# Chunk-band attention of layer 1: logits from split queries and keys, and late transposes in the output bank

## The reference

```python
def _band_attend(q, k, v, q_pos, k_pos, rel_table):
    rel = jnp.clip(q_pos[:, None] - k_pos[None, :], -REL_CLIP, REL_CLIP) + REL_CLIP
    bias = jnp.moveaxis(rel_table[rel], -1, 0).astype(F32)
    logits = jnp.einsum('bthd,bshd->bhts', q, k).astype(F32) * (DH ** -0.5) + bias[None]
    logits = jnp.where((k_pos >= 0)[None, None, None, :], logits, -jnp.inf)
    p = jax.nn.softmax(logits, axis=-1)
    return jnp.einsum('bhts,bshd->bthd', p.astype(v.dtype), v)
```

## Time and profile before

| what | value |
|---|---|
| median of the runs | 2955.19 us |
| the profiled execution | 2956.45 us, its span 2954.6 us, mean granted PE clock 0.98 |
| PE busy | 2824.2 us (96%) |
| POOL busy | 1530.0 us (52%) |
| attention of layer 1 | from 1913.72 us to about 2131 us of the span |

### The profile page before, as it was taken

How to read it: one execution, slowest core, us unless ns; L and a number is a source line. 1 busy time by engine, 2 the same in 40 slices (tenths; PEclk the granted TensorE clock), 3 DMA queues, 4 the chain that set the end, 5 groups by cost and what they waited for, 6 DMA issues and landing times. The chain is left out here.

```text
span 2954.6 us, 61044 instructions
## 1 busy us (share of the span) xinstructions
PE 2824.2 (96%) x24967; PEld 2635.7 (89%) x24967; DVE 1722.6 (58%) x3113; ACT 998.7 (34%) x2105; POOL 1530.0 (52%) x1382
## 2 busy tenths in 40 slices
PE   6999999997799999999999999999999999999998
PEld 4869999665699999999999999866699999999998
DVE  6389999556647633436797300066648544346785
ACT  3241111456525333333232201266525333333232
POOL 2222223664524877777576233144334777776675
PEclk8999999997999999999999999999999999999999
DMA  6736762733241122124322232263211222214322
GB/s 222 243 122 227 263 234 74 226 132 120 74 155 51 66 87 83 70 87 139 103 81 75 72 105 96 71 218 102 89 70 41 84 77 76 87 66 138 124 70 70
DMA packets 192389, 339.12 MB, mean 115 GB/s; under 512 B 27992, under 2 KB 107632, under 8 KB 190256
## 3 DMA queue, kind: packets, MB, share of 16 engines
q1 hardware_dynamic: 138832, 266.50, 26.9%
q10 hardware_dynamic: 53280, 68.72, 6.8%
HBM read 268.30 MB, written 79.49 MB: 118 GB/s over the span
## 5 line engine op out<-in xcount | busy, mean ns | idle before, releaser
L758 POOL TENSOR_TENSOR ah_ring_lo<-ah_raw,ah_ring_hi 128x512 fp32r<-128x512 f32 (+2 forms) x426 | 578.7, 1366 | 238.0 <-ACT ah_ring_hi L1182 146.9
L109 PE MATMUL tr_acc<-tr_quad_hi,ah_ring_hi 128*128 128x264 f32 x2432 | 694.5, 286 | 7.7 <-ACT tr_kept L1193 2.6
L111 PE MATMUL tr_acc<-tr_quad_hi,ah_ring_lo 128*128 128x264 f32 x2432 | 693.1, 285 | 0.0
L110 PE MATMUL tr_acc<-tr_quad_lo,ah_ring_hi 128*128 128x264 f32 x2432 | 690.7, 284 | 0.0
L109 PEld LDWEIGHTS tr_acc<-tr_quad_hi,ah_ring_hi 128*128 128x128 f32 x2432 | 458.6, 189 | 9.5 <-ACT tr_kept L1193 3.0
L110 PEld LDWEIGHTS tr_acc<-tr_quad_lo,ah_ring_hi 128*128 128x128 f32 x2432 | 458.6, 189 | 0.1
L111 PEld LDWEIGHTS tr_acc<-tr_quad_hi,ah_ring_lo 128*128 128x128 f32 x2432 | 458.2, 188 | 0.0
L1827 DVE TENSOR_SCALAR_CACHE_REDUCE f_q<-score,choose_trial 128x384 bf16<-128x384 f32 (+6 forms) x224 | 242.2, 1146 | 1.1
L3035 DVE CUSTOM_DVE_ANT_0 pc_prob<-pc_dots,pc_bias 128x640 f32<-128x640 f32 (+4 forms) x128 | 79.0, 655 | 273.3 <-PE pc_dots L2897 272.5
L2151 POOL CAST f_w_hi<-f_raw 128x512 fp32r<-128x512 f32 x66 | 44.5, 675 | 359.9 <-DMA f_raw<-in_w_dram 236.0
L756 POOL CAST ah_ring_hi<-ah_raw 128x512 fp32r<-128x512 f32 (+1 forms) x114 | 72.7, 638 | 279.4 <-PE tr_acc L111 258.6
(11 more groups left out here) (420 smaller groups left out, 7338.7 us busy)
## 6 DMA issues: line engine op xcount, KB each, us to landing
f_ada_w<-in_w_ada_dram SPq DMA_DIRECT2D x48, 1024.0 KB, 7.5
scratch_inner<-tr_kept ACTq DMA_DIRECT2D x88, 264.0 KB, 2.2
ah_raw<-in_w_gate_dram SPq DMA_DIRECT2D x44, 512.0 KB, 3.5
ah_raw<-in_w_up_dram SPq DMA_DIRECT2D x44, 512.0 KB, 4.4
ah_raw<-in_w_down_dram SPq DMA_DIRECT2D x64, 256.0 KB, 3.1
f_raw<-in_w_dram SPq DMA_DIRECT2D x24, 512.0 KB, 9.7
out_z_dram<-f_stage ACTq DMA_DIRECT2D x60, 176.0 KB, 2.0
out_z_dram<-tr_value ACTq DMA_DIRECT2D x48, 176.0 KB, 2.0
```

What stands on the lines that cost most here:

```text
L109: pe.matmul(out, w_hi, hi, start=start, stop=False, skip_group_check=onto)
L110: pe.matmul(out, w_hi, lo, start=False, stop=False, skip_group_check=onto)
L111: return pe.matmul(out, w_lo, hi, start=False, stop=stop, skip_group_check=onto)
L758: pool.tensor_tensor(lo[:, 0:width], own, hi[:, 0:width].bitcast(F32), ALU.subtract).then_inc(w_ready, 1)
```

## The change

Only the attention of layer 1 (`joined`) changes in what it does; for layer 0 the waits come out as they were.

- From pair 1 on q and k are split into `q_hi`, `k_hi` (rounded) and `q_lo`, `k_lo` (the rest, over the raw tensor). POOL does this in four parts for the next pair, one behind each `weigh` of i = 3 to 6: a cast of 128x512 and a subtraction of 128x512. `mask_band` comes behind the first part.
- `scores` becomes `split_scores` for these pairs: three fp32r products for each head. A 640-key tile goes in two pieces of 320 columns, one in each bank; a 128-key tile is computed 256 wide. The first tile of a pair waits for the fourth part of its split.
- The third group of transposes moves from step s+2, behind the values, to the head of step s+3, in front of the first two groups of the next tile, and goes into `out[0]`; ACT copies it out at once, at the head of its step. The first two groups go one to ACT and one to DVE for every tile.
- On DVE `inverse` of tile s-1 moves from ahead of both logits to between them, and `finish` moves from the end of the step to its head. The probability buffers go from three tiles to four. The sample keys and values have one buffer instead of four.

```diff
+            def split(g, n):
+                b, at = g % 2, slice(T // 2 * (n // 2), T // 2 * (n // 2) + T // 2)
+                raw, hi, lo = ((q, q_hi, q_lo), (k, k_hi, k_lo))[n % 2]
+                if n == 0:
+                    pool.wait_ge(qk_in[b], 32 * ((g + 1) // 2))
+                    if g >= 3:
+                        pool.wait_ge(dots_done, dots_after[step_of["tile", TILES * (g - 1) - 1]])
+                pool.tensor_copy(hi[b][:, at], raw[b][:, at]).then_inc(split_hi, 1)
+                pool.wait_ge(split_hi, 4 * (g - 1) + n + 1)
+                pool.tensor_tensor(lo[b][:, at], raw[b][:, at], hi[b][:, at].bitcast(F32), ALU.subtract).then_inc(split_lo, 1)
+                pool.wait_ge(split_lo, 4 * (g - 1) + n + 1)
...
                 for u, (g, i) in enumerate(units):
                     weigh(u)
+                    if 3 <= i < 7 and g < pairs - 1:
+                        pool.wait_ge(weighed, 2 * u + 2)
+                        split(g + 1, i - 3)
                     if i == 3 and g < pairs - 1:
                         pool.wait_ge(weighed, 2 * u + 2)
                         mask_band(g + 1)
...
+            def split_scores(s):
+                u = tile(s)
+                g, i = units[u]
+                b, n = g % 2, keys[i]
+                first = P * (i + 1) - n
+                wide_by = 320 if in_halves(s) else max(n, 256)
+                for piece in range(2 if in_halves(s) else 1):
+                    for p, (left, right) in enumerate(((q_hi, k_hi), (q_hi, k_lo), (q_lo, k_hi))):
+                        for hd in range(2):
+                            half = slice(DH * hd, DH * hd + DH)
+                            at = at_dots(s) + 512 * piece
+                            last = pe.matmul(dots[hd][:, at:at + wide_by], left[b][half, P * i:P * i + P],
+                                             right[b][half, first + wide_by * piece:first + wide_by * piece + wide_by],
+                                             start=p == 0, stop=p == 2)
+                last.then_inc(dots_done, 1)
...
                 if i == 0 and g:
-                    pe.wait_ge(qk_in[b], 32 * ((g + 1) // 2))
+                    if joined:
+                        pe.wait_ge(split_lo, 4 * g)
...
+                if turn_place[n] == 2 and i == 4:
+                    pe.wait_ge(finished, u // 4)
...
             for s in range(last_of + 5):
                 if tile(s) is not None:
                     scores(s)
...
+                for j in late_turns(s - 3) if joined else ():
+                    turns(s - 3, j)
                 for j in range(min(turns_of(s - 2), 2)):
                     turns(s - 2, j)
...
-                for j in range(2, turns_of(s - 2)):
+                for j in () if joined else late_turns(s - 2):
                     turns(s - 2, j)
...
-                if mask is None and summed is not None:
-                    inverse(summed)
+                if ends_quad(s - 4) and joined:
+                    finish(tile(s - 4) // 4)
                 if tile(s) is not None:
                     logit(s, 0)
...
+                if joined and summed is not None:
+                    inverse(summed)
                 if both_first:
                     logit(s, 1)
```

More of the change, by code:

```diff
@@ L2588, in attention_phase @@
     quads = side.quads + [(side.blocks, side.blocks + 1)]
+    joined = mask is None
+    depth = 4 if joined else 3
     steps = []
@@ L2613, in turns_of, with late_turns @@
         return len(quads) if group(s) is not None else 0
+    def late_turns(s):
+        return range(2, turns_of(s))
     def sums_of(s):
@@ L2633, in attention_phase @@
             by_act.append(False)
+        for j in late_turns(s - 3) if joined else ():
+            turn_no[s - 3, j] = len(by_act)
+            by_act.append(True)
         for j in range(min(turns_of(s - 2), 2)):
             turn_no[s - 2, j] = len(by_act)
-            by_act.append((item(s - 2)[1] + j) % 2 == 0)
+            by_act.append(j == 0 if joined and tile(s - 2) is not None else (item(s - 2)[1] + j) % 2 == 0)
         if group(s - 3) is not None:
@@ L2648, in attention_phase @@
             by_act.append(True)
+    late_no = {turn_no[s, j] for s in range(last_of) for j in late_turns(s)} if joined else set()
+    turn_place, turn_before, held, plain_turns = [], [], {}, 0
+    for n in range(len(by_act)):
+        place = 2 if n in late_no else plain_turns % 2
+        plain_turns += n not in late_no
+        turn_place.append(place)
+        turn_before.append(held.get(place))
+        held[place] = n
     act_no = [sum(by_act[:n]) for n in range(len(by_act) + 1)]
@@ L2881, in dots_free, with in_halves, halves @@
                 pe.wait_ge(logits, sums_before[s - 1])
+        def in_halves(s):
+            return joined and units[tile(s)][0] > 0 and keys[units[tile(s)][1]] == 640
+        def halves(ap, n):
+            return ap.rearrange("p (b n) -> p b n", n=n)[:, :, 0:320]
         @block.tensor
         def _(pe):
+            def split_scores(s):
[13 more added lines that the diff above has]
+                last.then_inc(dots_done, 1)
             def scores(s):
@@ L2992, in side_values @@
                             right = s_v_new[:, 256 * g + DH * j:256 * g + DH * j + DH]
-                        last = pe.matmul(turn[n % 2][S * j:S * j + S, 0:DH], left, right, start=c == 0, stop=c == side.blocks)
+                        last = pe.matmul(turn_at(n)[S * j:S * j + S, 0:DH], left, right, start=c == 0, stop=c == side.blocks)
                 last.then_inc(turned, 1)
@@ L3145, in _ @@
                 for j in own:
-                    if j >= 2:
+                    if j >= 2 and not joined:
                         copy(s - 2, j)
-                if ends_quad(s - 4):
+                if ends_quad(s - 4) and not joined:
                     finish(tile(s - 4) // 4)
@@ L3218, in _ @@
                 own = [j for j in range(turns_of(s - 2)) if by_act[turn_no[s - 2, j]]]
+                for j in late_turns(s - 3) if joined else ():
+                    copy(s - 3, j)
                 for j in own:
```

86 lines of the change are left out of this document (54 added, 32 removed).

## The result

| | this kernel | kernel before |
|---|---|---|
| median of the runs | 2973.99 us (4 runs, 2972.24 to 2980.28) | 2954.68 us (4 runs, 2953.36 to 2957.77) |
| the profiled execution | 2975.20 us, span 2973.3 | 2956.45 us, span 2954.6 |
| attention of layer 1, first scores to first product of the next phase | 241.06 us | 221.27 us |
| the rest of the span | 2732.2 us | 2733.3 us |

The ratio of the times is 1.0068, with a 95% interval of 1.0057 to 1.0080: slower by 19 us. The forecast was 2972.5 in a range of 2959 to 2981, so the time came out as predicted; how much of that is luck stands in the part on the prediction. The whole difference lies in the stage that the change touches: it grew by 19.8 us, and the rest of the span did not grow.

A forecast was written before the change was run, and what follows sets the result against it. PE was busy 96%, but POOL's chain of weighs and split parts was taken to decide: 2956.45 + 8.1 + 9.2 (clock) = 2973.8 us for the profiled execution, 1.3 above the median, so 2972.5; range 2959 to 2981.

The forecast's parts named there:

- POOL's chain: Weigh(3) to part 4 keeps POOL busy 14.7 us; next pair's scores start 19.5 us after those of i = 3.
- The clock: Behind four new PE stops of 3.7 to 3.9 us the clock halves, costing 2.3 us each, +9.2 us.
- The sum without the clock: Layer 1 attention: POOL's delays less PE and DVE gains, summed over pairs and tail, +8.1 us.
- tail: End of the layer 1 attention stage, with its late groups of transposes joined: -0.3 us.
- PE and DVE alone: Steps i = 0 to 7 of a pair, without POOL's limit, would take 24.1 us against 25.2 before.
- The prices of scores and subtractions: Split scores of 640 keys take 1.08 us instead of 1.28; a POOL subtraction 1.28 us rather than 1.43.
- (a): Rival: PE's stops are there but the clock holds, 2963 us; chance 0.14.
- (b): Rival: POOL keeps up, so scores and transposes bring what they save, 2945 us; chance 0.07.
- (c): Rival: POOL's chain is shorter by a quarter and loss and gain cancel, 2955 us; chance 0.08.
- (d): Rival: fp32r products of the two heads run one after the other, 2988 us or more; chance 0.06.

The follow-up runs named there:

- e1_fill: Changed kernel, with PE turning the identity 35 times before the first scores of pairs 1, 3, 5 and 7: 2969.47 us, stage 233.25 us.
- e2_cheap: Changed kernel with POOL's subtraction replaced by a cheaper copy, so logits are not the reference's: stage 220.02 us.
- e8_act_casts: Changed kernel with the split's casts on ACT and POOL's subtractions behind weigh(2) to weigh(5) (pair 0: 3, 4, 4, 5): 2943.17 us, ratio 0.9964 to kernel before.
- e6_all_spread: Changed kernel with split parts behind weighs of i = 1, 2, 4, 5, for pair 0 behind 3, 4, 4, 5: 2948.78 us, ratio 0.9978 to kernel before.
- e7_all_spread_ahead: As e6_all_spread, with POOL's split of the next phase's weights moved from i = 0 to i = 7: 2949.55 us, ratio 0.9982 to kernel before.
- e4_inverse: Changed kernel with DVE's inverse back ahead of both logits: 2969.77 us, stage 235.36 us.
- e3_spread: Changed kernel with split parts behind weighs of i = 1, 2, 4, 5 from pair 1 on, pair 0 left alone: 2954.73 us (one execution), stage 217.55 us.

## Why the prediction was right, and where its terms were off

**POOL's chain (right).** I had 14.7 us from the start of weigh(3) to the end of part 4; it took 15.0. I had 19.5 us from the scores of i = 3 to the next pair's; it took 19.72 (1976.33 to 1996.05). The stops before pairs 1, 3, 5 and 7 measured 3.83, 3.84, 3.83 and 3.82 us, where I had 3.7 to 3.9, and those before pairs 2, 4 and 6 0.13 each. All are ended by the subtraction at L2894. Of the 0.3 us between 14.7 and 15.0, 0.2 are my rounding: 1.36 + 2.07 + 0.5 and three times 1.58 + 2.07 make 14.9.

**The clock (right in kind, near in size).** Behind the four stops the first step took 5.60, 5.32, 4.65 and 4.65 us instead of 3.03, and behind the first stop the second took 0.35 more: 8.5 us in all, where I had 4 x 2.3 = 9.2. I took 4.6 us of work at half clock behind each stop. The half-clock stretches were 6.8 us long before pairs 1 and 3 and 3.4 before pairs 5 and 7, and they did not begin where PE took up work again. Before pair 3 the clock fell 1.7 us ahead of that, while PE stood still; before pair 5 it was still 1.00 through the whole stop and fell 0.8 us behind it (windows of the kernel after, as above):

```profile
1994.40:1996.00 1.60, 0.00 (x0) 0.00 (x0) 0.00 (x0) 0.00 (x0) 1.51 (x2) 0.50 0.64 248
2051.10:2054.80 3.70, 0.00 (x0) 0.00 (x0) 0.00 (x0) 0.15 (x2) 3.45 (x5) 1.00 0.82 322
```

So a single stop cost 1.6 to 2.9 us, and that the average came near my 2.3 is partly luck. e1_fill gives nearly the same number from the other side (7.8). That the clock falls behind each of these four waits is what the section that I cited from the Trainium skill ("TensorE: Matmul & The Clock Gate", "HAM oscillation — how this bites in real kernels") says of a loop that waits in each round, and here the trace agrees. The waits of its example are longer than the stops of e2_cheap, 1.63 to 1.88 us, and behind those the clock fell in two of four.

**The sum without the clock (undersized).** It was to be +8.1 us and is 19.8 - 8.5 = +11.3. From the starts of each pair's first scores in both timelines, the clock's share taken off:

| | forecast | measured |
|---|---|---|
| pair 0 | +2.0 | +3.7 |
| pairs 2, 4, 6, each | +3.0 | +3.4 |
| pairs 1, 3, 5, each | -0.5 | -0.25 |
| pair 7 | -1.1 | -1.4 |
| tail | -0.3 | -0.4 |

The largest miss of a single pair is pair 0. I added the chain to pair 0's weigh(3) where the trace of before has it. But the move of `inverse` holds in pair 0 too and costs it 1.2 us: weigh(3) starts 2.40 us after the scores of i = 4 (1919.16 to 1921.56), in the kernel before 1.18 us (1921.53 to 1922.71). For the other pairs I had counted this move. Its step i = 3 was 0.15 us longer too. The rest is the chain, 0.3 us longer each time, and turns that wait for a late weigh: i = 7 of an odd pair takes 3.93 us, where I had 3.82, and i = 0 behind the sample step 3.50. The sample step itself was forecast right (3.9, measured 3.92).

**Luck in the total.** The stage was to grow by 17.3 us and grew by 19.8: 3.2 more without the clock, 0.7 less through it. The profiled execution came out 1.4 us above my 2973.8 and not 2.5, because the rest of its span happened to be 1.1 us shorter, and two misses in the stage went against each other. The mechanism was right; the closeness of the total is partly chance.

**PE and DVE alone (right, seen in e8_act_casts).** With POOL out of the way the steps of an ordinary pair take 3.03, 3.03, 2.88, 2.43, 2.88, 2.91, 3.12 and 3.56 us, 23.8 in all; I had 24.1. The inverse between the logits I priced at 0.15 us; in i = 4 it costs 0.07. DVE's timeline of the kernel after shows this: the reciprocal starts together with the read of the accumulator, and the second logit 0.07 us behind both, before the 0.16 us of the reciprocal are over.

```profile
1980.70 0.08 DVE L3120 DVE_READ_ACCUMULATOR2_ANT pc_least<- 128x1 f32 x1
1980.70 0.16 DVE L3138 RECIPROCAL pc_inv<-pc_sum 128x2 f32<-128x2 f32 x1
1980.77 0.80 DVE L3120 CUSTOM_DVE_ANT_0 pc_prob<-pc_dots,pc_bias 128x640 f32<-128x640 f32 x1
```

Where the reciprocal has to wait for ACT's row sum it costs more: in i = 5 of the same pair the logits start 1.06 us apart (1982.83 to 1983.89) instead of 0.75. The values of i = 2 wait 0.26 us for the copy of the late transposes (forecast 0.34); that step came out at its forecast all the same, and why i = 3 is 0.07 shorter than forecast stays open. The 9 to 10 us of gain that I had for this case are 10.0 in e8_act_casts, but not pair by pair: pairs 2 to 7 gain 1.4 to 1.7 us each, where I had 1.1 to 1.4, and pair 1 gains nothing because of its stop.

**The prices of scores and subtractions (right).** Scores of 640 keys hold PE 1.08 us (1988.21 to 1989.29). The subtraction takes 1.26 to 1.29 us and not 1.43, as the row of the same stage had it in the earlier trace rows. The rule on the shared port in the Trainium skill ("SBUF — State Buffer", "SBUF: two separate sides") spoke for this, and the trace agrees. What makes 1.43 of it elsewhere, no run here tested.

**The rivals.** (a), the clock holds, falls by the windows and by e1_fill. (b), POOL keeps up, falls for this kernel, but its time, 2945 us, is about what e8_act_casts reaches by making it nearly true (2943.17). (c), loss and gain cancel, wanted a chain shorter by a quarter; in e2_cheap, with 2.6 of its 15.0 us off, they cancel already (stage 1.2 us below before). (d), heads one after the other, falls: pairs of 64-row products follow each other by 0.145 us at 320 columns (the price that I had for one), and each pair is both heads.

## What to carry to other kernels

Add up the engine that gets the new work in order of time between two fixed points, and not over the stage: POOL was busy 53% of the span, 63% of the stage (151 of 241 us), and still the last to finish in every pair that had a split. A move that delays the start of such a chain (`inverse` behind a logit) has to be charged wherever the chain runs, the first round included. Work with slack behind it belongs where an engine has idle time: against the kernel with the moves alone, the split costs 24.8 us on POOL behind i = 3 to 6, the clock behind its stops included; it gains 0.6 to 1.9 us on POOL when it is spread earlier, and 5 us with its casts on ACT.

## What the runs showed of the hardware that I had not expected

- **Short stops of PE can cost the clock, but not each time.** A stop of 1.63 us was followed by a granted clock of 0.50 in e6_all_spread, and not in e7_all_spread_ahead or e2_cheap; in e2_cheap 1.81 and 1.88 us were followed by it and 1.86 was not; in e4_inverse 2.66 us was not, and 3.05, 3.09 and 3.17 were. In e8_act_casts 1.59 us was not. All four of 3.82 to 3.84 us in the kernel after were, and the 3.85 in e3_spread. Half clock then lasted 3.4 or 6.8 us, which is 1.3 to 1.6 or 2.3 to 2.9 us of lost work; behind the pause of 2.46 us at the head of the stage it lasted 6.8 us in ten of the eleven traces and 10 in e4_inverse. What decides between them, no run here shows.
- **Useless work can pay.** 35 transposes of the identity in a stop of 3.8 us kept the clock at 1.00 and saved about 2 us each time (e1_fill). Moving the work that made the stop was worth far more (e3_spread, 23.5 us).
- **fp32r products of 64 rows for two heads run side by side,** 0.145 us for both at 320 columns, as plain fp32 products do; the kernel before had no row for it.
